# Computing the modulation in quarters beside the first two projection groups, with GpSimd taking two of sixteen row sums

## The chip, the cores and the metric

One core of a Trainium2 chip. The metric is the device time of one launch in microseconds (us), the median of several executions. The engines are named as the profile names them: PE (TensorE), DVE (VectorE), ACT (ScalarE), POOL (GpSimd), SP (the queue that issues most transfers).

## What is computed

Two transformer blocks over 256 tokens of width 2048. The change touches the start of the first and two details later. All weights are float32 in HBM, and every matrix product is to have float32 precision.

```python
mod = silu(c) @ ada_w + ada_b                  # c: 2048 values, ada_w: 2048 x 6144
shift, scale, gate = split(mod, 3)
h = rms_norm(x, norm_g) * (1.0 + scale) + shift
proj = h @ w_in                                # 2048 x 9296, in groups of 512 columns
```

Then follow rotations, a recurrence (forget gates from the first 1024 columns computed), an index score (16 heads of 64), a top-64 selection, attention, an output projection, and a second block with a long convolution, attention and a feed-forward layer.

## The kernel before

**Products.** `Gemm` cuts each product in groups of 512 columns, each group in chunks of 512 rows (1 MB, one transfer from SP into one of the four places of `raw`), each chunk in two parts. A part is numbered through the whole kernel. For each part ACT rounds the weights (`high`, L399), DVE takes the remainder (`low`, L408), and PE makes 12 matmuls of 512 columns (`multiply_group`, L430): three products of halves for two row tiles and two token tiles. `w_hi` holds four parts, so ACT and DVE are at most four parts ahead of PE. Two pairs of PSUM banks (`ps`) are used in turns by even and odd groups; a group starts when the group two before it has been read out. Work beside the products is written as generators that yield the number of the part at which they may go on (`GATE_AT`, `INDEX_AT`, `TAPS_AT` and others), and `Spare` hands it out after each part.

**Modulation (the start).** Shift and scale are 4096 columns, so `n_ada` = 8 steps g of 512 columns, in order of columns. Each step streams 2048 rows of `ada_w` as four 1 MB chunks c = 0..3 through the same four places of `raw` (SP, L2199 and L2203; `ada_free` says when a place is free). A chunk holds four row sums: a weight row tile times four columns of `c_sig`. PE makes nine of the sixteen itself (c = 0, c = 2 and the first of c = 3, stationary operand one column wide, L511), DVE makes the other seven into `mod_part` (L1149, L1151), and PE adds that up over the partitions with a column of ones. ACT copies the row out (`mod_row`, L1857) and PE turns it into columns with four tiny matmuls (128 columns of a row each). DVE has `before_products` beside it: the rotation angles and their sine, the normalised rows (`normalise`, L1023), the lower bounds of the forget gate (`lb`, L1113 to L1133). PE turns three units of normalised rows (L523) between steps.

After the last step DVE adds the bias (L1163), ACT makes the input tiles `h_hi` from PSUM with scale and shift (`tile_of_first`, L1793), DVE their lower halves (`low_of_first`, L967), and PE starts with part 0; parts 0 to 7 are group 0, 8 to 15 group 1. Only when the last `ada_w` chunks are used does SP load `w_in`.

**Later.** `gate_row` streams the gate's third of `ada_w` in 16 chunks from ACT's queue, beside the products, 64 operations on DVE (L1182). The index scores are 16 steps of two matmuls over 64 partitions (`kiT`, `qiT`); even steps use partitions 0 to 63, odd ones 64 to 127. The filter taps are eight matmuls over 64 partitions, four on the lower half, then four on the upper one, two at each part. The recurrence's `inside` makes three such matmuls per head, two on the lower and then one on the upper 64 partitions. GpSimd makes only the filter's first layer (L2265), which starts when the recurrence is over.

## Time and profile before

| what | value |
|---|---|
| median of 3 runs (lowest, highest) | 2101.46 us (2100.26, 2109.39) |
| the profiled execution itself | 2106.29 us |
| its span in the trace | 2104.5 us |
| mean granted clock of PE | 0.986 |
| busy: PE, DVE, ACT, POOL | 2058.0, 1302.7, 927.1, 383.0 us |
| moved by DMA | 408.47 MB, mean 194 GB/s |

Times inside the trace are counted from the start of the span. The busy time of an engine is no limit by itself: the stage in which it waits has to be looked up.

### The profile page before, as it was taken

What the parts mean: (1) busy time and instruction counts of PE and PEld (TensorE: products, weight loads), DVE (VectorE), ACT (ScalarE), POOL (GpSimd) and SP (SyncE); (2) the same over time, 40 slices, a digit from 0 to 9 for tenths busy, and PEclk for the clock granted to TensorE, in tenths of its full rate; (3) what the DMA queues carried; (4) which work ended last, traced back from release to release, by engine and by line L of the source; (5) the groups of instructions that cost most, each with busy time, mean ns of one, the idle gap of its engine ahead of it and who ended that gap; (6) DMA issues with size and microseconds to landing.
All of it is one profiled execution on the core that took longest, in us unless ns stands there. A gap on an engine that the chain in (4) does not pass through costs nothing.

```text
span 2104.5 us, 23568 instructions
## 1 busy us (share of the span) xinstructions
PE 2058.0 (98%) x9245; PEld 1623.4 (77%) x9245; DVE 1302.7 (62%) x1651; ACT 927.1 (44%) x1224; POOL 383.0 (18%) x588
## 2 busy tenths in 40 slices
PE   6989999999999999999999999999999999999999
PEld 1268787777887888786788888888888888878887
DVE  4857667798666678865765666554544544444443
ACT  1165523455654544354454434554444444433332
POOL 0000002999999950000000000000000000000000
PEclk9999989999999999999999999999999999999999
DMA  9967557555565675554435555555555555546554
GB/s 353 344 236 249 199 185 220 180 171 164 171 213 196 200 231 180 160 163 130 138 129 186 187 198 180 180 194 187 191 188 186 194 186 194 194 166 199 186 195 160
DMA packets 205683, 408.47 MB, mean 194 GB/s; under 512 B 10826, under 2 KB 12163, under 8 KB 204931
## 3 DMA queue, kind: packets, MB, share of 16 engines
q1 hardware_dynamic: 190480, 376.07, 54.1%
q10 hardware_dynamic: 13332, 24.40, 3.4%
q0 software_dynamic: 1760, 6.49, 1.5%
q8 instruction: 73, 1.20, 0.2%
q14 instruction: 38, 0.31, 0.0%
HBM read 404.83 MB, written 2.10 MB: 193 GB/s over the span
## 4 chain that ended last, share of the span: by engine, by line
PE 91%; DVE 6%; DMA 2%; issue 1%; ACT 0%; ACTq 0%; SPq 0%; DVEq 0%
PE ps L430 81%; PE pm L511 6%; DMA raw<-in_ada_w 2%; DVE raw_lo L408 1%; PE ps L511 1%; PE pm L523 1%; DVE mod_part L1151 1%; PE pm L575 1%; PE pm L888 0%; DVE gate L1182 0%; DVE xtmp L1351 0%; DVE sc_i L1268 0%; DMA rows_b<-in_hgrn_norm_g 0%; DVE proj L1328 0%; PE pm L710 0%
## 5 line engine op out<-in xcount | busy, mean ns | idle before, releaser
L408 DVE TENSOR_TENSOR raw_lo<-raw,w_hi 128x1024 fp32r<-128x1024 f32 (+1 forms) x648 | 799.9, 1238 | 597.6 <-ACT w_hi L399 589.0
L399 ACT ACTIVATE w_hi<-raw 128x1024 fp32r<-128x1024 f32 (+1 forms) x648 | 680.1, 1050 | 821.0 <-PE ps L430 796.3
L430 PE MATMUL ps<-w_hi,h_hi 128*128 128x512 f32 (+1 forms) x2336 | 941.3, 403 | 12.5 <-DVE raw_lo L408 6.4
L430 PE MATMUL ps<-w_hi,h_lo 128*128 128x512 f32 (+1 forms) x2336 | 912.5, 391 | 0.0
L430 PE MATMUL ps<-raw_lo,h_hi 128*128 128x512 f32 (+1 forms) x2336 | 911.2, 390 | 0.0
L430 PEld LDWEIGHTS ps<-w_hi,h_hi 128*128 128x128 f32 x2336 | 442.8, 190 | 117.3 <-issue 13.0
L430 PEld LDWEIGHTS ps<-raw_lo,h_hi 128*128 128x128 f32 x2336 | 443.3, 190 | 93.3 <-issue 7.7
L430 PEld LDWEIGHTS ps<-w_hi,h_lo 128*128 128x128 f32 x2336 | 442.2, 189 | 93.4
L2265 POOL TENSOR_TENSOR proj<-proj 128x128 f32<-128x128 f32 x264 | 177.8, 679 | 12.9
L2265 POOL TENSOR_TENSOR proj<-proj,w1T 128x128 f32<-128x128 f32 x165 | 102.8, 631 | 11.4 <-DMA proj<-in_z 4.2
L430 PE MATMUL ps<-w_hi,hid_hi 128*128 128x512 f32 x256 | 100.6, 393 | 2.0 <-DVE raw_lo L408 2.0
L430 PE MATMUL ps<-raw_lo,hid_hi 128*128 128x512 f32 x256 | 100.3, 392 | 0.0
L430 PE MATMUL ps<-w_hi,hid_lo 128*128 128x512 f32 x256 | 100.2, 391 | 0.0
L2244 POOL DMA_DIRECT2D proj<-in_z x22 | 14.1, 645 | 344.4 <-DVEq L1246 338.7
L511 PE MATMUL ps<-raw,c_sig 128*1 128x512 f32 x144 | 70.2, 638 | 6.7 <-DMA raw<-in_ada_w 6.5
L430 PEld LDWEIGHTS ps<-w_hi,hid_hi 128*128 128x128 f32 x256 | 48.3, 189 | 12.3 <-DVE raw_lo L408 2.2
L511 PEld LDWEIGHTS ps<-raw,c_sig 128*1 128x1 f32 x144 | 11.5, 87 | 59.5 <-issue 47.0
L430 PEld LDWEIGHTS ps<-w_hi,hid_lo 128*128 128x128 f32 x256 | 48.5, 189 | 10.1
L430 PEld LDWEIGHTS ps<-raw_lo,hid_hi 128*128 128x128 f32 x256 | 48.4, 189 | 10.0
L1182 DVE SCALAR_TENSOR_TENSOR gate<-proj,c_sig,gate 128x512 f32<-128x512 f32 x64 | 49.1, 767 | 1.9
L2265 POOL TENSOR_TENSOR proj<-h3T,proj 128x128 f32<-128x128 f32 x66 | 48.9, 742 | 0.0
L1151 DVE SCALAR_TENSOR_TENSOR mod_part<-raw,c_sig,mod_part 128x512 f32<-128x512 f32 x48 | 36.0, 750 | 10.2 <-DMA raw<-in_ada_w 8.6
(308 smaller groups left out, 1183.5 us busy)
## 6 DMA issues: line engine op xcount, KB each, us to landing
raw<-in_w_in SPq DMA_DIRECT2D x140, 1024.0 KB, 5.2
raw<-in_w_ffn_gate SPq DMA_DIRECT2D x44, 1024.0 KB, 5.2
raw<-in_w_ffn_up SPq DMA_DIRECT2D x44, 1024.0 KB, 5.2
raw<-in_w_ffn_down SPq DMA_DIRECT2D x44, 1024.0 KB, 5.2
raw<-in_ada_w SPq DMA_DIRECT2D x32, 1024.0 KB, 7.7
raw<-in_w_out SPq DMA_DIRECT2D x32, 1024.0 KB, 5.2
proj<-in_ada_w ACTq DMA_DIRECT2D x16, 1024.0 KB, 5.3
raw<-in_w_br_hyena SPq DMA_DIRECT2D x8, 1024.0 KB, 5.2
```

Source lines behind the costliest of these rows:

```text
L399: nc.scalar.activation(w_hi[:, p % HRING, :, 0:gm.width(j)], raw[:, k % RING, e:e + HT, 0:gm.width(j)], ACT.Copy).then_inc(hi_done, 1)
L408: nc.vector.tensor_tensor(raw_lo[:, k % RING, e:e + HT, 0:gm.width(j)], raw[:, k % RING, e:e + HT, 0:gm.width(j)], w_hi[:, p % HRING, :, 0 ...
L430: mm = nc.tensor.matmul(ps[pair][:, t, 0:gm.width(j)], l[:, tok], r[:, i, 0:gm.width(j)], start=(k == 0 and q == 0), stop=(k == kt - 1 and ...
L511: return nc.tensor.matmul(o, l, r, start=start, stop=stop, **kw)
L523: i = nc.tensor.transpose(b[:, ((k % 2) * TT + t) * P:((k % 2) * TT + t + 1) * P], src[:, t, k * P:k * P + P], ident[:])
L575: i = nc.tensor.transpose(b[:, o:o + P], src[:, t, h * HD:h * HD + HD], ident[:])
L1151: i = v.scalar_tensor_tensor(mod_part[:, g % 2], raw[:, c, k], w_, mod_part[:, g % 2], ALU.mult, ALU.add)
L1182: x = v.scalar_tensor_tensor(acc, gate_raw[i % 2][:, k], c_sig[:, CK * c + k:CK * c + k + 1], acc, ALU.mult, ALU.add)
L2244: pool.dma_start(z_k[e % 2][half * HID:half * HID + HID], z.partition_broadcast(HID)).then_inc(sig(f"z_in{e % 2}"), 16)
L2265: g.tensor_tensor(o, x, y, op).then_inc(sig("sum_step"), 1)
```

## The change

The `w_in` groups 0 and 1 advance together: for each quarter q of the 2048 inputs, the steps g = 2q (shift) and g = 2q + 1 (scale) of the modulation are computed, and then the four parts of quarter q of both groups. The parts are renumbered (`part` with `together`: 0, 1 of group 0, 2, 3 of group 1, and so on).

- `ada_w` chunks go to four places of their own in `proj` (`ada_raw`); SP issues the `w_in` chunk of group 0 behind c = 0 and that of group 1 behind c = 1 of each odd g.
- Row sums of a step: PE five of sixteen (c = 0 and the first of c = 2), POOL two (the first two of c = 1: two multiplications and an addition of 128x512), DVE nine and one addition of POOL's sum.
- PE's queue, for g even: sums of c = 0, turn the previous quarter's two rows (eight tiny matmuls), sum of c = 2, the ones matmul behind `mod_parts`, two parts of that quarter. For g odd: c = 0, a part, c = 2, a part, the ones matmul; in the last step both parts come after it. The whole normalised input is turned at g = 2 and copied by ACT into `h1_raw`.
- DVE's queue: for g even, the columns of the quarter (`columns_of`) behind c = 1, a `low_of_first` behind c = 2 and c = 3; for g odd, the `low` of four parts behind c = 3. `before_products` has lost the angles; they go as `rotation_angles` beside groups 2 and 3. The gate's chunks start at part 22 instead of 12 and end at 78 as before.
- The index matmuls of two steps are issued together, alternating between the lower and the upper 64 partitions; the taps alternate too.

```diff
-ADA_PE = 1
+PE_C2 = 1
+POOL_C1 = 2
-GATE_AT = [12 + 22 * i // 5 for i in range(4 * ADA_GATE)]
+GATE_AT = [22 + 56 * i // 15 for i in range(4 * ADA_GATE)]
...
+        if self.together and j < 2 and n < self.parts:
+            return self.n0 + 2 * PARTS * (n // PARTS) + PARTS * j + n % PARTS
...
+        ada_raw = [proj[:, 1, o:o + CK * GW].rearrange("p (k n) -> p k n", k=CK) for o in (A_Q, A_V, R_Q, R_I)]
...
+            if c % 2 == 0:
+                sp.wait_ge(ada_used, 2 * (g - 1) + 1 + c // 2)
+            if c:
+                sp.wait_ge(mod_parts, 3 * (g - 1) + c)
+            if c == 1:
+                sp.wait_ge(sig("pool_sums"), g)
...
             for g in range(n_ada):
+                q = g // 2 - 1
+                if g == 2:
+                    pe.wait_ge(sig("h1_rows"), 1)
+                    for u in range(KT // 2):
+                        b = bank(pe, ("h1", u), "a")
...
+                row_sums(g, 0, CK, sums)
+                if q >= 0:
+                    if g % 2 == 0:
+                        turn_modulation(q, mods)
+                    elif g < n_ada - 1:
+                        early_part(4 * q + 2)
+                row_sums(g, 2, PE_C2, sums)
+                if q >= 0 and g % 2 and g < n_ada - 1:
+                    early_part(4 * q + 3)
+                pe.wait_ge(mod_parts, 3 * g + 3)
+                mm(sums[0:1, :], ones[:, 0:1], mod_part[:, g % 2], start=False, stop=True).then_inc(filled, 1)
+                if q >= 0:
+                    if g % 2 == 0:
+                        early_part(4 * q)
+                        early_part(4 * q + 1)
+                    elif g == n_ada - 1:
+                        early_part(4 * q + 2)
+                        early_part(4 * q + 3)
+            q = n_ada // 2 - 1
+            turn_modulation(q, bank(pe, ("mods", q), "v"))
+            for p in range(2 * g_in.parts - 4, 2 * g_in.parts):
+                early_part(p)
...
-                    for j in range(IDX_H // 2):
-                        yield INDEX_AT[1 + t] + j
+                    for j in range(0, IDX_H // 2, 2):
+                        yield INDEX_AT[1 + t] + j + 1
...
+                        for q in range(2):
+                            for r in range(2):
+                                part = slice(IDX_D * r, IDX_D * r + IDX_D)
+                                m = mm(b[r][:, q * SEQ:q * SEQ + nk], qiT[part, j + q, t * P:t * P + P], kiT[part, 0:nk])
...
-                    t, n = i // 4, i % 4
+                    t, n = i % TT, i // TT
...
+                for c, k0 in ((1, POOL_C1), (2, PE_C2), (3, 0)):
+                    dve.wait_ge(ada_landed[c], 16 * (g + 1))
...
+                            if last:
+                                dve.wait_ge(sig("pool_sums"), g + 1)
+                                v.tensor_tensor(mod_part[:, g % 2], mod_part[:, g % 2], pool_part[g % 2], ALU.add).then_inc(sig("pool_added"), 1)
...
+                    if q >= 0 and g % 2 == 0:
+                        if c == 1:
+                            columns_of(q)
+                        else:
+                            low_of_first(2 * q + c - 2)
+                    if g % 2 and c == 3:
+                        for p in range(4 * (g // 2), 4 * (g // 2) + (2 if g == n_ada - 1 else 4)):
+                            low_of(p)
+                    early.step(g, 3.0 if g < 2 else 1.2)
+            for p in range(2 * g_in.parts - 2, 2 * g_in.parts):
+                low_of(p)
+            columns_of(n_ada // 2 - 1)
+            for u in (KT // 2 - 2, KT // 2 - 1):
+                low_of_first(u)
...
+            groups(g_in, (2, 3), None, ((chain, 1e9), (angles, 1.6), (gate_work, 1.0)))
...
-            for c in range(RING):
-                sp.dma_start(raw[:, c], ada_v[:, CK * c:CK * c + CK, 0:GW]).then_inc(landed[c], 16)
-            for g in range(1, n_ada):
+            for g in range(n_ada):
+                o = D * (g % 2) + GW * (g // 2)
                 for c in range(RING):
-                    ada_free(sp, g, c)
-                    sp.dma_start(raw[:, c], ada_v[:, CK * c:CK * c + CK, GW * g:GW * g + GW]).then_inc(landed[c], 16)
+                    if g:
+                        ada_free(sp, g, c)
+                    sp.dma_start(ada_raw[c], ada_v[:, CK * c:CK * c + CK, o:o + GW]).then_inc(ada_landed[c], 16)
+                    if g % 2 and c < 2:
+                        load(sp, g_in, c, g // 2)
...
+            def row_part(g_):
+
+                pool.wait_ge(ada_landed[1], 16 * (g_ + 1))
...
+                for k, o in ((0, pool_part[g_ % 2]), (1, pool_part[2])):
+                    g.tensor_tensor(o, ada_raw[1][:, k], c_sig[:, CK + k:CK + k + 1].to_broadcast([P, GW]), ALU.mult).then_inc(sig("pool_step"), 1)
+                pool.wait_ge(sig("pool_step"), 2 * (g_ + 1))
+                g.tensor_tensor(pool_part[g_ % 2], pool_part[g_ % 2], pool_part[2], ALU.add).then_inc(sig("pool_sums"), 1)
```

## Rows read from the trace of the kernel before

**Rows 1.** The page: busy time of the engines over the span.
```profile
PE 2058.0 (98%) x9245; PEld 1623.4 (77%) x9245; DVE 1302.7 (62%) x1651; ACT 927.1 (44%) x1224; POOL 383.0 (18%) x588
```

**Rows 2.** Windows: length; PE, PEld, DVE, ACT, POOL busy; PE clock, DMA share, GB/s.
```profile
40.00:80.00 40.00, 36.18 (x108) 9.56 (x108) 34.33 (x56) 7.02 (x8) 0.00 (x0) 1.00 1.03 372
...
90.00:100.00 10.00, 10.00 (x23) 2.06 (x22) 6.48 (x6) 0.35 (x1) 0.00 (x0) 0.85 0.58 203
...
160.00:210.00 50.00, 50.00 (x226) 40.80 (x225) 35.94 (x38) 26.42 (x28) 0.00 (x0) 0.97 0.72 248
...
290.00:300.00 10.00, 10.00 (x60) 8.26 (x60) 7.38 (x12) 2.30 (x3) 0.00 (x0) 0.50 0.37 127
...
360.00:410.00 50.00, 46.32 (x193) 35.56 (x192) 45.08 (x51) 20.88 (x35) 46.85 (x60) 1.00 0.65 209
```

**Rows 3.** Timeline of PE at the start: start, us, instruction, idle before it.
```profile
63.69 3.59 PE L511 MATMUL ps<-raw,c_sig 128*1 128x512 f32 x8
...
99.54 1.05 PE L511 MATMUL ps<-ones,mod_row 1*128 1x1 f32 x8
...
100.52 0.66 PE L523 MATMUL pm<-ident,hbuf 128*128 128x128 f32 x4
...
111.70 1.02 PE L511 MATMUL ps<-mod_part,ones 128*1 128x512 f32 x2 [0.69 <-DVE mod_part L1151]
...
120.61 0.79 PE L430 MATMUL ps<-w_hi,h_hi 128*128 128x512 f32 x1 [5.43 <-DVE h_lo L967]
...
123.33 0.60 PE L430 MATMUL ps<-w_hi,h_hi 128*128 128x512 f32 x1
```

**Rows 4.** The chain that ended last: one part of a group.
```profile
125.53 2.76 PE ps L430 x12
```

**Rows 5.** Timeline of DVE at the start.
```profile
36.90 2.33 DVE L1151 SCALAR_TENSOR_TENSOR mod_part<-raw,c_sig,mod_part 128x512 f32<-128x512 f32 x3 [1.10 <-DMA raw<-in_ada_w]
...
45.98 2.61 DVE L1023 TENSOR_SCALAR hbuf<-x_res,hs 128x2048 f32<-128x2048 f32 x2
...
91.12 3.35 DVE L1126 RECIPROCAL xtmp<-xtmp 128x512 f32<-128x512 f32 x1
...
109.32 2.33 DVE L1151 SCALAR_TENSOR_TENSOR mod_part<-raw,c_sig,mod_part 128x512 f32<-128x512 f32 x3 [2.10 <-DMA raw<-in_ada_w]
...
114.70 0.19 DVE L1163 TENSOR_TENSOR mod_cols<-ps,cols 128x32 f32<-128x32 f32 x1 [3.05 <-PE ps L511]
...
115.25 4.63 DVE L408 TENSOR_TENSOR raw_lo<-raw,w_hi 128x1024 fp32r<-128x1024 f32 x4
...
119.80 0.76 DVE L967 TENSOR_TENSOR h_lo<-xtmp,h_hi 128x256 fp32r<-128x256 f32 x2
```

**Rows 6.** Timeline of ACT: an input tile, and the read-out of group 1.
```profile
117.04 0.54 ACT L1793 ACTIVATE xtmp<-pm,mod_cols,g_col 128x256 f32<-128x256 f32 x1
...
167.85 1.03 ACT L1888 ACTIVATE proj<-ps 128x1024 f32<-128x1024 f32 x1 [1.60 <-PE ps L430]
```

**Rows 7.** The page: transfers of w_in, KB each, median us from issue to landing.
```profile
raw<-in_w_in SPq DMA_DIRECT2D x140, 1024.0 KB, 5.2
```

**Rows 8.** Timeline of PE: matmuls over 64 partitions; each matmul is two instructions.
```profile
321.74 0.71 PE L511 MATMUL pm<-proj 64*128 64x128 f32 x6
...
423.99 0.71 PE L511 MATMUL pm<-kiT,qiT 64*128 64x128 f32 x4
...
481.26 1.13 PE L511 MATMUL pm<-kiT,qiT 64*128 64x256 f32 x4
...
875.52 1.98 PE L511 MATMUL pm<-gate,h3T 64*128 64x512 f32 x4
```

**Rows 9.** Groups by line: POOL; then DVE within 200 to 340 us.
```profile
L2265 POOL TENSOR_TENSOR proj<-proj,w1T 128x128 f32<-128x128 f32 x165 | 102.8, 631 | 11.4 <-DMA proj<-in_z 4.2
...
L1182 DVE SCALAR_TENSOR_TENSOR gate<-proj,c_sig,gate 128x512 f32<-128x512 f32 x36 | 27.0, 749 | 1.1
```

**Rows 10.** Groups by line: the same DVE line within 360 to 400 us.
```profile
L1182 DVE SCALAR_TENSOR_TENSOR gate<-proj,c_sig,gate 128x512 f32<-128x512 f32 x8 | 7.1, 890 | 0.2
```

More of the change, by code:

```diff
@@ L128, in part, with done @@
     def part(self, j, n=0):
+        if self.together and j < 2 and n < self.parts:
+            return self.n0 + 2 * PARTS * (n // PARTS) + PARTS * j + n % PARTS
         return self.n0 + self.parts * j + n
+    def done(self, j):
+        return self.part(j, self.parts - 1) + 1
     def end(self):
@@ L205, in build @@
         sn_rope = sb("sn_rope", [P, 5, 2 * TT * 96], F32, st)
+        mod_row = sb("mod_row", [P, 2, GW], F32, st)
+        mod_part = sb("mod_part", [P, 2, GW], F32, st)
         st.close()
@@ L334, in build @@
         landed = [sem(f"landed{i}") for i in range(RING)]
+        ada_landed = [sem(f"ada_landed{i}") for i in range(RING)]
         ada_used = sem("ada_used")
@@ L555, in _, with row_sums @@
-            pe.wait_ge(sig("mod_read"), n_ada + 2)
-            for j in range(4 * (n_ada - 1), 4 * n_ada):
-                m = mm(mod_bank[:, j:j + 1], mod_row[0:1, j * P:j * P + P], ones[0:1, 0:1])
-            m.then_inc(sig("mod_turned"), 1)
+            def row_sums(g, c, n, b):
+                pe.wait_ge(ada_landed[c], 16 * (g + 1))
+                for k in range(n):
+                    m = mm(b[0:1, :], c_sig[:, CK * c + k:CK * c + k + 1], ada_raw[c][:, k], start=(c == 0 and k == 0), stop=False)
+                m.then_inc(ada_used, 1)
@@ new lines, in turn_modulation, with early_part @@
+            def turn_modulation(q, b):
+                for r in range(2):
+                    drained(("mod", 2 * q + r))
+                    for i in range(CK):
+                        m = mm(b[:, CK * r + i:CK * r + i + 1], mod_row[0:1, r, i * P:i * P + P], ones[0:1, 0:1])
+                m.then_inc(filled, 1)
+            def early_part(p):
+                n = 2 * (p // 4) + p % 2
+                pe.wait_ge(sig("first_lo"), n + 1)
+                multiply_part(pe, g_in, p % 4 // 2, n, halves)
@@ L735, in _ @@
             beside = Chains(mixer, gate_sum)
-            def turn_h1(n):
-                if n + 3 < KT // 2:
-                    turn_unit("h1", hbuf, n + 3)
-                drained(("h1", n))
-            for j in range(g_in.groups):
-                multiply_group(pe, g_in, j, halves, turn_h1 if j == 0 else None, beside if j else None)
+            for j in range(2, g_in.groups):
+                multiply_group(pe, g_in, j, halves, None, beside)
             multiply(pe, g_o, halves, made("mix"), beside)
@@ L1162, in _ @@
[L1162 to L1171 removed]
+                            dve.wait_ge(mod_parts, 3 * g + c)
@@ L1418, in _ @@
             gate_sum = Spare(gate_sums())
+            groups(g_in, (2, 3), None, ((chain, 1e9), (angles, 1.6), (gate_work, 1.0)))
+            assert angles.over
             beside = ((chain, 1e9), (gate_sum, 1e9), (gate_work, 1.0), (head_work, 1.2))
-            groups(g_in, range(1, g_in.groups), None, beside)
+            groups(g_in, range(4, g_in.groups), None, beside)
             assert gate_work.over and head_work.over and gate_sum.over
@@ L2035, in _ @@
             beside = ((chain, 1e9), (norm_work, 1.2), (gate_work, 1e9))
-            groups(g_in, range(1, g_in.groups), read_in, None, beside)
+            groups(g_in, range(2, g_in.groups), read_in, None, beside)
             assert norm_work.over and gate_work.over
```

279 lines of the change are left out of this document (145 added, 134 removed).

## The prediction, made before the changed kernel was run

> **What bounds the kernel now.** The page comes first: PE is busy for 2058.0 of 2104.5 us [rows 1], so outside the places where PE waits only fewer or shorter matmuls can save anything. The windows say where it waits. From 40 to 80 us the DMA share is 1.03 at 372 GB/s, with PE busy for 36.2 and DVE for 34.3 of 40 us: the modulation runs at the rate of the transfers, and both engines are nearly full beside it [rows 2]. Between 90 and 100 us the share falls to 0.58 while PE is busy throughout at a clock of 0.85: there PE's sums hold the places of the ring. The timeline gives the end of the stage: DVE gets the last chunk at 109.3 us [rows 5], PE's first product starts at 120.6 after 5.43 us of idleness, and it runs at the lower clock until 123.3 [rows 3]; ACT reads group 1 out at 167.85 [rows 6]. So the start costs 120 us ahead of the products, and groups 0 and 1 end at 167.7. Everything behind that is PE's, but for a stretch like 360 to 410 us, where PE is busy for 46.3 and DVE for 45.1 of 50 us: DVE is late there [rows 2].
>
> **Prices.** One 1 MB chunk at 372 GB/s takes 2.8 us [rows 2]; alone, it lands 5.2 us after its issue [rows 7]. Four row sums on PE take 3.6 us, one 0.9, the ones matmul 1.0, the four tiny turning matmuls 1.0, a transposed unit 0.66 [rows 3]; a part is 2.76 us [rows 4]. On DVE three sums are 2.33 us, a `low` 1.16, a `low_of_first` 0.76, the columns with their gaps some 0.5 (from 114.70 to 115.25), the rows' normalisation 2.61, half a reciprocal 1.65 [rows 5]. An ACT tile operation lasts 0.54 us, and four make a unit, 1.85 us as they overlap a little [rows 6]. The addition of POOL's sum is not in the trace: I take 0.7 us, between nothing and the 0.75 of a three-operand one [rows 9], so that DVE's four sums and the addition are 3.8 us, and 4.1 with POOL beside them.
>
> **DMA.** In place of 4 chunks a step there are 10 a pair of steps (8 of `ada_w`, 2 of `w_in`): 28.2 us a pair. Nothing is removed, 8 MB are moved ahead of the last `ada_w` chunk: 8 x 2.8 = 22.5 us more of transfers. In return up to ten of the sixteen parts, 27.6 us, lie beside them. The floor of the exchange is therefore a gain of a few us and not of 27.
>
> **The first pair.** DVE's last sums of step 1 start at 36.9 now [rows 5]; two `w_in` chunks ahead put that at 42.5. The early work behind c = 2 (normalisation, reciprocal and a 1.16 us maximum, 4 us) holds DVE from 42.3 to 46.3, so the sums end at 50.4 and the ones matmul at 51.4. Then PE turns all eight units at once (6 us, paced by ACT's copies) and does c = 0 of step 2: S = 61.
>
> **A pair in steady state.** I follow PE from the end of the c = 0 sums of an even step (S) to the same point one pair on. PE turns eight tiny matmuls (2.0), DVE makes the columns (0.5), the three sums of c = 2 (2.33), a `low_of_first` (0.8) and the sums of c = 3 (4.1); PE makes the ones matmul (1.0), two parts (5.5), c = 0 of the odd step (3.6), a part (2.76), a sum (0.9), a part (2.76), the ones matmul (1.0) and c = 0 again (3.6): 30.8 us. Ahead of the even ones matmul PE has been idle for some 7 us. After 5.43 us of idleness it needed 2.7 us for what takes half of that [rows 3], so 1.3 us come on top: 32.1 us. This is longer than the 28.2 us of the transfers, so **the chain PE, DVE, PE sets the pair and no longer the DMA**; `columns_of` stands ahead of the c = 2 sums on DVE, and c = 0 of the odd step, which SP waits for to reload, stands behind two parts on PE. S for step 6 is 61 + 64.2 = 125.2.
>
> **The end of the stage.** Steps 5 to 7 also carry the lower bounds' reciprocals, two of 1.65 us in this chain: mod_parts of step 6 at 138.2, ones and two parts with the clock 146.1, c = 0 and c = 2 of step 7 at 150.5 (the last chunk, issued at 138.2, lands at 143.4 and is summed by 147.5, so it does not decide). Then ones (151.5), parts 10 and 11 (157.0), `high` and `low` of part 15 which stand ahead of the columns (159.2), columns, an input tile, its lower half (162.3), and the four parts of the last quarter: groups 0 and 1 end at 173.3, **5.6 us later than now**. SP's reload of `raw` behind them waits for parts 10 to 15 in turn and lands ahead of its use.
>
> **POOL.** Its 128x128 operation takes 0.63 us [rows 9]; for 512 columns that bounds it by 0.63 and 2.5 us. I take 1.4, by the ratio of DVE's 512 and 128 columns in the same class of work being about two: 4.2 us for three, 7.6 at the upper end. Either lies inside a step of 16 us and delays no reload. What it costs is DVE's speed: the same DVE sum took 749 ns with POOL idle and 890 ns with POOL at work [rows 9, 10], 19% more. POOL works for a quarter of a step, early in it, hence my 0.3 us a step. The Trainium skill's GPSIMD Engine Reference, Key points, says that POOL shares its SBUF interfaces with VectorE and contends with instructions that have two SBUF inputs, which is nearly everything DVE does here; the trace agrees. If all sums of the chain paid 19%, it would be 1.2 us a pair and 3.6 us in all, so 9 and not 5.6 us.
>
> **Beside groups 2 and 3.** The angles come to DVE here, 10.9 us by the shares in their generator. DVE is busy for 35.9 of 50 us between 160 and 210 [rows 2], so 14 us are free, and the first gate chunks (operations of 0.75 us) leave it. It fits, barely: 1 us, bounds 0 and 3. The gate's sixty-four operations then stand closer together (16 chunks in 56 parts, not 66); where DVE already is late, 360 to 410 us, that is one or two operations of 0.89 us: 1 us, bounds 0 and 2.
>
> **The 64-partition matmuls.** Two matmuls of 128 columns (four instructions) last 0.71 us and two of 256 columns 1.13, so 0.42 is for columns and 0.29 fixed. Three matmuls of the recurrence, of which the last uses the other 64 partitions, are six instructions and also last 0.71 us, where 0.92 would be due one after the other [rows 8]: the third was hidden. By that, joined steps cost what one costs: the index saves 4 x 0.71 + 4 x 1.13 less tails, some 6.6 us, the taps 4 x (1.98 - 1.13), 3.4 us: 10 us. The lower bound is the fixed part alone, eight times 0.29, 2.3 us. PE is the bound at both places, so it counts.
>
> **Sum.** +5.6 + 1 + 1 - 10 = -2.4 us against the profiled execution (span 2104.5, time 2106.29, itself 4.8 above the median). Taken off the median of 2101.46: **2099 us**. A change under 0.5%, 10.5 us, is about what a measurement of this kernel can't tell from none.
>
> **Rivals.**
> - *The transfers keep the pace* (0.20). The engines' chain slips beside them, each pair takes 28.2 us: last chunk at 42.5 + 84.6 = 127.1, then 4.1 + 1.0 + 5.5 + 2.2 + 0.5 + 1.85 + 0.8 + 11.0 = 26.9 us, end at 154, 13.7 us earlier; in all -22 us: 2080. For it: the share of 1.03 now. Against: DVE's columns wait for PE in each pair, and nothing in the order written out lets either pass.
> - *Matmuls over alternate halves don't overlap* (0.13): 2.3 us saved in place of 10, 2107. For it: only one pair of three shows it.
> - *The clock stays down in the stage* (0.12), slower. PE now waits in short stretches every pair; granted half speed lasted beyond them (0.85 at 90 to 100 us with PE busy throughout, 0.50 for all of 290 to 300 [rows 2]). A pair holds some 24 us of PE's work. My sum has 2.7 us of it at the lower clock. Each further 2 us cost 1; if half of the work is at the lower clock, 5 us a pair beyond mine come on, 15 in all, 2114. It turns slower by 0.5% from some 11 us a pair at half speed.
> - *The overlap fails* (0.05): a part's `high` waits for a part that PE issues behind the sums, so that the parts run as a block. Up to ten parts come back, and 22.5 us of transfers stay: 2120 to 2125.
> - *My forecast* (0.50), its own range 2092 to 2107.
>
> **Numbers.** Faster by over 0.5%: the first rival, and the lower edge of my forecast, 0.27. Slower: the clock and the failed overlap in most of their cases, 0.12. Within: 0.61. The range reaches from the first rival to the middle of the third, 2080 to 2113.
>
> **What would show it.** Right: S near 61 and 93, groups 0 and 1 read out at 172 to 175 us, DMA share about 0.9 from 60 to 140 us, PE idle ahead of the ones matmul of even steps for 5 to 8 us and DVE idle ahead of `columns_of`; index rows of eight instructions at about 0.71 and 1.13 us; DVE sums at 0.75 to 0.89. Wrong: a read-out ahead of 160 us, a share of 1.0 throughout, joined rows at 1.1 and 2.0 us, or a waits view in which POOL's sum holds DVE.

## The result and the profile after

The changed kernel takes 2120.9 us (median of nine runs, 2114.67 to 2124.03), the kernel before 2104.34 on the same chips (nine runs, 2098.67 to 2109.39). The ratio is 1.0075, 95% interval 1.006 to 1.0089: **slower by three quarters of a per cent**, where 2099 us and no measurable change were forecast, and outside the range of 2080 to 2113. The profiled execution took 2117.41 us with a span of 2115.6, so the two traces differ by 11.1 us and the medians by 16.5. The profile of before is 2 us above its median, that of after 3.5 below; the account below is of the 11.1.

The page of the changed kernel: busy times, and the group of PE's products that waits.
```profile
PE 2028.8 (96%) x9181; PEld 1615.9 (76%) x9181; DVE 1334.2 (63%) x1683; ACT 932.5 (44%) x1232; POOL 415.0 (20%) x612
...
L440 PE MATMUL ps<-w_hi,h_hi 128*128 128x512 f32 (+1 forms) x2336 | 945.1, 405 | 20.4 <-DVE raw_lo L423 15.8
```
PE is busy for 29 us less than in [rows 1]: 64 instructions fewer are 32 row sums at 0.9 us. Yet the span is longer, so PE is idle for 86.8 us in place of 46.5. DVE is busy for 31.5 us more. By design it has two sums and an addition more in each step than before, which are 18 us (16 sums of 0.75 us, and 6.2 us of additions); where the rest comes from is the subject of the second experiment.

The timeline of PE from 50 to 170 us, only the rows of the modulation and of the waits:
```profile
52.04 1.87 PE L529 MATMUL pm<-mod_part,ones 128*1 128x512 f32 x2 [10.84 <-DVE mod_part L1218]
...
62.15 1.94 PE L529 MATMUL pm<-ones,mod_row 1*128 1x1 f32 x16
...
71.41 1.87 PE L529 MATMUL pm<-mod_part,ones 128*1 128x512 f32 x2 [6.37 <-DVE mod_part L1218]
...
95.19 1.94 PE L529 MATMUL pm<-ones,mod_row 1*128 1x1 f32 x16
...
104.44 1.87 PE L529 MATMUL pm<-mod_part,ones 128*1 128x512 f32 x2 [6.36 <-DVE mod_part L1218]
...
128.69 1.94 PE L529 MATMUL pm<-ones,mod_row 1*128 1x1 f32 x16
...
139.60 1.86 PE L529 MATMUL pm<-mod_part,ones 128*1 128x512 f32 x2 [8.02 <-DVE mod_part L1218]
...
153.77 1.02 PE L529 MATMUL pm<-mod_part,ones 128*1 128x512 f32 x2 [0.68 <-DVE mod_part L1218]
...
166.03 0.80 PE L440 MATMUL ps<-w_hi,h_hi 128*128 128x512 f32 x1 [3.71 <-DVE h_lo L1016]
```
The starts of the `ones,mod_row` rows are the prediction's S: 62.15, 95.19 and 128.69, forecast 61, 93.1 and 125.2. The pairs last 33.0 and 33.5 us, not 32.1, and PE waits 6.4 to 8.0 us ahead of each even ones matmul, which takes 1.87 us after that idleness and 1.02 in the odd steps, after a wait of 0.68 us or none.

ACT's timeline has the read-out of group 1, which answers to 167.85 in [rows 6]:
```profile
180.07 1.03 ACT L1980 ACTIVATE proj<-ps 128x1024 f32<-128x1024 f32 x1 [1.09 <-PE ps L440]
```
So groups 0 and 1 end 12.2 us later than before; 5.6 was forecast. Windows of the same kernel, with columns as in [rows 2]:
```profile
60.00:140.00 80.00, 59.25 (x201) 29.36 (x199) 62.62 (x79) 25.91 (x38) 16.30 (x12) 0.84 0.85 306
...
202.00:210.00 8.00, 7.93 (x32) 6.53 (x32) 7.83 (x10) 3.25 (x3) 0.00 (x0) 0.79 0.27 80
```
The columns are the length, the busy times of PE, its weight loads, DVE, ACT and POOL, then the clock, the DMA share and GB/s. The DMA share of 0.85 shows that the transfers no longer pace the stage; the engine that is fullest is DVE. The granted clock of 0.84 was 0.91 in the same window before.

**Where the time came from.** I subtracted the start of the same part's first product in the timelines of PE (part 16: 167.7 before, 179.9 after). Worked out from the traces, us later than before:
```
part                       0     8    16    24    84   120   236   252   end
the changed kernel     -47.4  -4.5 +12.2 +17.1 +15.7 +16.4 +15.4 +11.2 +11.1
without POOL's sums    -48.9  -7.8  +6.3  +9.9 +10.3 +11.6  +9.0  +6.4  +6.4
```
The second row is that of an experiment below. The early start is real (part 0 is 47.4 us ahead), and by part 16 all of it is gone. 4.9 us more go in group 2. Over the index steps (parts 84 to 120) the offset first falls, to +11.0 at part 112, and is back at +16.4 by part 120, so nothing net is gained. 4.2 come back in the stretch with the taps (236 to 252). How these stand to the terms forecast comes after the experiments.

### The profile page after: what moved, and what is told of

Its sections match the earlier page's. It is cut to its first block, busy times and chain, and to the rows that moved or that the text cites. A ratio compares the mean times of both kernels' runs of the same rounds, so it can differ in the third digit from the quotient of the medians.

```text
span 2115.6 us, 23544 instructions
## 1 busy us (share of the span) xinstructions
PE 2028.8 (96%) x9181; PEld 1615.9 (76%) x9181; DVE 1334.2 (63%) x1683; ACT 932.5 (44%) x1232; POOL 415.0 (20%) x612
## 4 chain that ended last, share of the span: by engine, by line
PE 89%; DVE 8%; DMA 1%; issue 1%; ACT 1%; ACTq 0%; SPq 0%; DVEq 0%
PE ps L440 79%; PE pm L529 7%; DVE raw_lo L423 2%; DVE mod_part L1218 1%; DMA proj<-in_ada_w 1%; PE pm L541 1%; PE pm L628 1%; DVE sc_i L1338 0%; PE pm L938 0%; DVE xtmp L1421 0%; DVE gate L1252 0%; ACT w_hi L414 0%; DMA rows_b<-in_hgrn_norm_g 0%; DVE proj L1163 0%; PE pm L585 0%
## 5 line engine op out<-in xcount | busy, mean ns | idle before, releaser
L1218 DVE SCALAR_TENSOR_TENSOR mod_part<-proj,c_sig,mod_part 128x512 f32<-128x512 f32 x64 | 52.9, 827 | 9.6 <-DMA proj<-in_ada_w 7.6
L529 PE MATMUL pm<-mod_part,ones 128*1 128x512 f32 x16 | 12.4, 869 | 38.5 <-DVE mod_part L1218 38.5
L529 PE MATMUL pm<-proj,c_sig 128*1 128x512 f32 x80 | 40.5, 642 | 8.6 <-DMA proj<-in_ada_w 8.6
```

The source lines that it names most:

```text
L529: return nc.tensor.matmul(o, l, r, start=start, stop=stop, **kw)
L1218: i = v.scalar_tensor_tensor(mod_part[:, g % 2], ada_raw[c][:, k], w_, mod_part[:, g % 2], ALU.mult, ALU.add)
```

## The experiments

Each ratio below is against the kernel before on the same chip. Single ratios carry some 0.0015 either way, so the traces decide on terms of a few us, and where the two disagree it is said.

### Alternate taps alone

```diff
-                    t, n = i // 4, i % 4
+                    t, n = i % TT, i // TT
```
This is the kernel before with that one edit, on PE and on DVE.

> The kernel before with one edit: the eight filter-tap matmuls alternate between the lower and the upper 64 partitions. If alternate halves overlap, the stretch with the taps is 3.4 to 4 us shorter in the trace (part 236 to 252) and four instructions that lasted 1.98 us last about 1.1; total 2100. Rival, that the 4.1 us that the changed kernel won in that stretch come from somewhere else (other buffers, the clock): no difference, 2104.

Measured: 2103.42 us (ten runs), ratio 1.0001 (0.9986 to 1.0017). The timeline of PE in it:
```profile
873.17 1.13 PE L511 MATMUL pm<-gate,h3T 64*128 64x512 f32 x4
```
1.13 us in place of 1.98 [rows 8]: the halves overlap. Four such groups are 3.4 us, which this ratio does not show. So it was run again:

> The kernel of before_taps once more, with more rounds, since its trace was 5.7 us shorter in the stretch with the taps and its median was not. If the 3.4 us of four steps (1.98 to 1.13 us) stay, the ratio is 0.998 to 0.9985. If something later takes them back in unprofiled executions, it is 1.000 again.

Measured: 2101.32 us, ratio 0.9983 (0.9966 to 1.0), which is the 3.4 us forecast, at the edge of what twelve runs can tell. The traces are clearer. From the first of the four groups to the transposes behind the last it is 22.45 us in the kernel before and 19.1 in every kernel with alternate taps: 3.4 us each time. The stretch from part 236 to 252 is longer and differs less evenly, by 5.7 us in the first run and 2.5 in the second, because behind the taps the clock was low for a while before (0.86 from 925 to 950 us), not at all in the first run (1.00) and again in the second (0.86). Two kernels below differ by the taps as well.

### POOL's row sums

```diff
-POOL_C1 = 2
+POOL_C1 = 0
-                                dve.wait_ge(sig("pool_sums"), g + 1)
-                                v.tensor_tensor(mod_part[:, g % 2], mod_part[:, g % 2], pool_part[g % 2], ALU.add).then_inc(sig("pool_added"), 1)
```
SP's wait for POOL and the calls of POOL's `row_part` are gone too; DVE makes eleven of the sixteen sums.

> The changed kernel with POOL's two row sums of each step back on DVE, its addition gone. Theory 1 (the chain through PE, DVE and the low clock sets the stage): DVE has two sums more and one addition less, 0.8 us a step, but its c = 1 sums, 2.8 to 3.0 us for two beside POOL, go at 0.75 each again, so four take as long as two; groups 0 and 1 end within 1.5 us of 179.9, total 2119 to 2122. Theory 2 (POOL's slowing of DVE is what the stage lost against the forecast): the sums behind it also get faster, groups 0 and 1 end at 174 to 176, total 2116 or less. Theory 3 (POOL does help): the stage is 4 us or more longer.

Measured: 2112.21 us (four runs), ratio 1.0053 (1.0038 to 1.0068). Its row in the table above stands 5.9 us below the changed kernel's at part 16. **With more sums on DVE, the stage is shorter.** Its S are 61.40, 94.10 and 125.83, near the forecast's 61, 93.1 and 125.2.

The groups of DVE by line within 20 to 165 us, first of the changed kernel:
```profile
L1218 DVE SCALAR_TENSOR_TENSOR mod_part<-proj,c_sig,mod_part 128x512 f32<-128x512 f32 x60 | 49.9, 832 | 7.5 <-DMA proj<-in_ada_w 5.6
...
L423 DVE TENSOR_TENSOR raw_lo<-raw,w_hi 128x1024 fp32r<-128x1024 f32 x16 | 20.6, 1320 | 7.8 <-ACT w_hi L414 7.7
...
L1211 DVE TENSOR_SCALAR mod_part<-proj,c_sig 128x512 f32<-128x512 f32 x7 | 7.9, 1126 | 13.9 <-DMA proj<-in_ada_w 13.9
...
L1216 DVE TENSOR_TENSOR mod_part<-mod_part,proj 128x512 f32<-128x512 f32 x8 | 6.2, 781 | 0.3
```
The same groups without POOL's sums:
```profile
L1214 DVE SCALAR_TENSOR_TENSOR mod_part<-proj,c_sig,mod_part 128x512 f32<-128x512 f32 x74 | 55.4, 749 | 9.1 <-DMA proj<-in_ada_w 6.9
...
L421 DVE TENSOR_TENSOR raw_lo<-raw,w_hi 128x1024 fp32r<-128x1024 f32 x16 | 19.0, 1222 | 9.8 <-ACT w_hi L412 9.7
...
L1209 DVE TENSOR_SCALAR mod_part<-proj,c_sig 128x512 f32<-128x512 f32 x7 | 3.2, 456 | 15.8 <-DMA proj<-in_ada_w 15.8
```
Add them: 84.6 us of DVE with POOL's help, 77.6 without. POOL takes 14 sums, 10.5 us; the addition gives 6.2 back; the rest, 84.6 - (77.6 - 10.5 + 6.2) = 11.3 us, is what DVE loses while POOL works beside it. The mean of 832 ns hides where. The timelines of both engines of the changed kernel, in step 4, DVE first:
```profile
92.00 2.04 DVE L423 TENSOR_TENSOR raw_lo<-raw,w_hi 128x1024 fp32r<-128x1024 f32 x1 [2.61 <-ACT w_hi L414]
93.97 1.26 DVE L1211 TENSOR_SCALAR mod_part<-proj,c_sig 128x512 f32<-128x512 f32 x1
95.26 1.64 DVE L1218 SCALAR_TENSOR_TENSOR mod_part<-proj,c_sig,mod_part 128x512 f32<-128x512 f32 x1
...
91.92 1.04 POOL L2370 TENSOR_TENSOR proj<-proj,c_sig 128x512 f32<-128x512 f32 x1 [15.10 <-issue]
...
92.92 2.02 POOL L2370 TENSOR_TENSOR proj<-proj,c_sig 128x512 f32<-128x512 f32 x1
...
95.02 1.32 POOL L2372 TENSOR_TENSOR proj<-proj 128x512 f32<-128x512 f32 x1
```
and the same DVE work without POOL:
```profile
90.91 1.22 DVE L421 TENSOR_TENSOR raw_lo<-raw,w_hi 128x1024 fp32r<-128x1024 f32 x1 [2.61 <-ACT w_hi L412]
92.05 0.48 DVE L1209 TENSOR_SCALAR mod_part<-proj,c_sig 128x512 f32<-128x512 f32 x1
92.57 2.33 DVE L1214 SCALAR_TENSOR_TENSOR mod_part<-proj,c_sig,mod_part 128x512 f32<-128x512 f32 x3
```
Beside POOL the `low` takes 2.04 in place of 1.22 us, the first sum 1.26 in place of 0.48, the next 1.64 in place of some 0.77: 1.7 to 2.6 times as long, for as long as POOL's three operations of 512 columns last. The rows read as if the two engines took turns: the `low` ends at 94.04, 1.08 us after POOL's first product (92.96), POOL's second product then ends 0.90 later (94.94) and has taken 2.02 us where the first took 1.04, and each DVE operation ends a fraction of its own time after POOL's. That they take turns is my reading of the times; no run tests it. Not every DVE operation is slowed. The first reciprocal of step 6 lies beside POOL's operations, which last from 125.36 to 129.72, and takes as long as the next one with POOL idle, 1.75:
```profile
127.41 1.74 DVE L1163 RECIPROCAL proj<-proj 128x256 f32<-128x256 f32 x1
```

Is it contention, or the waits and the addition? The next kernel keeps POOL's products, its sum (in steps 0 to 6) and SP's wait (which costs SP 0.3 us in all), but DVE makes all eleven sums and uses none of it. POOL's part of the edit, against the changed kernel:
```diff
-            for g_ in range(n_ada):
+            for g_ in range(n_ada - 1):
                 row_part(g_)
```

> The kernel after_nopool (DVE makes all eleven sums), but in steps 0 to 6 POOL makes its two products and their sum all the same, into memory that nobody reads; SP's reload of c = 1 waits for them as in the changed kernel. If POOL's work slows DVE's, groups 0 and 1 end 5 to 8 us later than the 173.9 of after_nopool, and the c = 1 sums beside POOL's work take 1.3 to 1.4 us in place of 0.49 and 0.75; total 2118 to 2121. If the changed kernel lost the time by its addition and the wait for POOL's sum, it ends at 173 to 175, total 2112.

Measured: groups 0 and 1 end 11.6 us later than before, not 6.3, and DVE's rows within 20 to 165 us are:
```profile
L1216 DVE SCALAR_TENSOR_TENSOR mod_part<-proj,c_sig,mod_part 128x512 f32<-128x512 f32 x74 | 63.3, 856 | 4.4 <-DMA proj<-in_ada_w 2.2
...
L423 DVE TENSOR_TENSOR raw_lo<-raw,w_hi 128x1024 fp32r<-128x1024 f32 x16 | 20.4, 1321 | 6.3 <-ACT w_hi L414 6.1
...
L1211 DVE TENSOR_SCALAR mod_part<-proj,c_sig 128x512 f32<-128x512 f32 x7 | 7.1, 1019 | 16.4 <-DMA proj<-in_ada_w 16.4
```
The same instructions as without POOL now take 90.8 us, 13.2 more. So in the traces **POOL's mere presence costs the stage 5.3 us**, near all of the 5.9. The medians don't confirm it: 2115.47 us is again a ratio of 1.0053 (1.0037 to 1.0068), because the kernel before was slower there (2105.5, against 2100.96 beside the kernel without POOL's sums). By ratio, POOL's sums cost 0.0022 in all, with overlapping intervals. I take the traces, where both the durations and the end of the stage agree. They don't stand alone either. Of the kernels in this document that keep the changed kernel's order of parts, the five with POOL at work (this one, the changed one, and those with the angles, the index and the fill edited) start part 16 10.7 to 13.4 us behind before's, and the three without it 5.5 to 6.4. And one pair of whole times is clear of its intervals: with the angles spread in both, 1.0053 (1.0033 to 1.0074) with POOL's sums and 1.0011 (0.9998 to 1.0024) without, the second also with the index as before, which by itself gained nothing.

### The angles over three groups

```diff
-            groups(g_in, (2, 3), None, ((chain, 1e9), (angles, 1.6), (gate_work, 1.0)))
+            groups(g_in, (2, 3, 4), None, ((chain, 1e9), (angles, 0.8), (gate_work, 1.0)))
```


> The changed kernel with the rotation angles spread over groups 2 to 4 at half the share a part (0.8 in place of 1.6). If DVE's load by the angles makes the 5 us that the changed kernel loses between parts 16 and 24, the wait of 3.0 us at 202 us goes and part 24 starts 3 to 5 us earlier; total 2117. Rival, that those 5 us are the low clock carried over from the start and the read-out of both groups at once: 0 to 1 us, total 2121.

Measured: 2112.74 us (four runs), ratio 1.0053 (1.0033 to 1.0074). Its parts 16 and 24 both stand 10.7 us behind before's; the changed kernel's stand 12.2 and 17.1 behind. The 4.9 us of group 2 are gone, the other 1.5 differ ahead of any edit and are spread between executions. The traces of the other kernels agree: with the angles crowded into groups 2 and 3 the six that were taken lose 3.6 to 6.0 us between parts 16 and 24, and the five with the angles spread lose 0.0. The 3.6 is that of the kernel without POOL's sums, so POOL isn't needed for this loss. (The profile of this run is another 6 us shorter where a low clock between parts 52 and 56 came out shorter; that isn't the edit's.)

What the angles do there, in the timeline of PE and the chain of waits of the changed kernel:
```profile
202.07 0.50 PE L440 MATMUL ps<-w_hi,h_hi 128*128 128x512 f32 x1 [2.97 <-DVE raw_lo L423]
```
```profile
182.38 1.22 DVE raw_lo L423
183.60 1.15 DVE proj L1267
...
184.78 0.57 DVE sn_rope L996
...
199.22 0.76 DVE gate L1252
...
200.79 1.24 DVE raw_lo L423
...
202.07 2.33 PE ps L440 x6
```
From 182.38 to 202.03 us the chain is DVE without a break: remainders, `proj` work of the forget gate, angles, gate. DVE falls behind, PE waits 2.97 us and then runs at a clock of 0.79 over 8 us (the window above), which is 1.7 us more: together 4.7 of the 4.9 us. The 0 to 3 us forecast counted the wait and not what the wait does to the clock.

### The index matmuls as before

PE's order (one step after the other) and the yields of ACT and DVE go back to those of the kernel before:
```diff
-                    for j in range(0, IDX_H // 2, 2):
-                        yield INDEX_AT[1 + t] + j + 1
+                    for j in range(IDX_H // 2):
+                        yield INDEX_AT[1 + t] + j
```


> The changed kernel with the index matmuls, and the part numbers of ACT and DVE for them, as before. Theory 1 (DVE is the bound from part 92 to 120, so what PE saves there comes back as a wait, and the shift by one part makes a new one of 4.7 us): without the edit the offset to the kernel before stays within 1 us from part 84 to part 128, where the changed kernel goes from +15.7 down to +11.0 and up to +16.4; total 2120, no difference. Theory 2 (the edit saves the 6.6 us forecast, and the wait at part 116 has another cause): the offset rises by 4 to 6 us to +20, total 2126.

Measured: 2121.96 us (four runs), ratio 1.009 (1.0073 to 1.0107), beside the changed kernel's 1.0075. Its parts stand 21.1 us behind before's at 84 and 21.0 at 120, and never more than 0.3 from that between them. The changed kernel's 15.7 and 16.4 are nearly the same at both ends, with the dip to 11.0 between. So the saving is made and then lost. The joined steps themselves last just what was forecast:
```profile
442.42 0.71 PE L529 MATMUL pm<-kiT,qiT 64*128 64x128 f32 x8
...
494.75 1.13 PE L529 MATMUL pm<-kiT,qiT 64*128 64x256 f32 x8
```
Eight instructions in the time of four [rows 8]. Its waits within 425 to 545 us (us in total, times, longest) and the chain ahead of the longest:
```profile
PE ps L440 <- DVE raw_lo L423: 8.3, 4, 4.7
```
```profile
518.07 0.61 DVE sc_i L1338
...
521.70 1.71 DVE xtmp L1421 x2
...
524.57 1.37 DVE raw_lo L423
```
With the index as before the same wait is 1.7 us, once. Ahead of the longest wait the chain is DVE's, from 513.45 to 525.94 us, busy for 12.6 of 13 us from 513 to 526: the scores, the search for the top 64 and the rotations stand ahead of the remainder that PE waits for. So 6.6 us less on PE came back as 6.6 us more of waits, 8.3 less 1.7. DVE's share over the whole stretch, 101.6 of 120 us busy, would not have told this by itself (see the taps below). The two kernels' whole times don't differ beyond their intervals.

### The parts moved into the waits

PE waits 6 to 8 us ahead of the even ones matmul, and makes two parts in a row behind it. Here the last two parts of the quarter before go ahead of that matmul, and the first two stand around the sums of the odd step:
```diff
                 row_sums(g, 2, PE_C2, sums)
-                if q >= 0 and g % 2 and g < n_ada - 1:
-                    early_part(4 * q + 3)
+                if q >= 0 and g % 2:
+                    early_part(4 * q + 1)
+                if q >= 1 and g % 2 == 0:
+                    early_part(4 * q - 2)
+                    early_part(4 * q - 1)
```
The rounding and the remainders of these parts move with them.

> The changed kernel with the parts in other places of PE's queue: the first two parts of a quarter around the sums of the following odd step, the last two in the wait ahead of the ones matmul of the next even step. Nothing is added or removed. Theory 1 (the chain sets the pair, 33 us, with 6 to 8 us of PE idle in it and the clock falling): PE's idle time is filled, the clock stays up, a pair takes 28 to 30 us, groups 0 and 1 end at 167 to 171, total 2109 to 2113. Rival (the transfers or DVE set the pair): the pair stays at 33 us, total 2120.

Measured: 2119.51 us (four runs), ratio 1.0084 (1.0058 to 1.0109), no gain in the whole time. Its timeline of PE:
```profile
62.83 1.94 PE L529 MATMUL pm<-ones,mod_row 1*128 1x1 f32 x16
...
89.48 1.94 PE L529 MATMUL pm<-ones,mod_row 1*128 1x1 f32 x16
...
114.47 1.87 PE L529 MATMUL pm<-mod_part,ones 128*1 128x512 f32 x2 [4.44 <-DVE mod_part L1217]
...
121.27 1.94 PE L529 MATMUL pm<-ones,mod_row 1*128 1x1 f32 x16
```
The first pair is 26.7 us, shorter than the 28.2 that the transfers were priced at; the next is 31.8 again, with PE waiting for DVE, which from step 5 on has the reciprocals of the lower bounds. So the order fills PE's gap once, and then DVE is late. Even so the stage is shorter: part 16 stands 8.2 us behind before's, 4.0 less than in the changed kernel. Behind it this profile has more low clock: the granted clock is 0.83 from 195 to 225 us and 0.76 from 280 to 330, where the changed kernel's is 0.89 and 0.83. That is some 5 us, and the end is 1.3 us later than the changed kernel's. The second of these clocks differs between profiles whatever the order of the parts (0.76 to 0.93), so the whole time of four runs says little about the order itself.

### Matmuls that keep the clock up

Matmuls with a column of zeros as weights fill PE's waits, `FILL = (0, 6, 5, 0, 5, 0, 5, 3)` of them in the eight steps; they add nothing to the sums:
```diff
                 row_sums(g, 2, PE_C2, sums)
+                for _ in range(FILL[g]):
+                    mm(sums[0:1, :], zcol[:, 0:1], x_res[:, 0, 0:GW], start=False, stop=False)
```


> The changed kernel with extra matmuls behind PE's c = 2 sum (stationary operand zero, so they add nothing): six in step 1, five in steps 2, 4 and 6, three in step 7. They fill the waits ahead of the ones matmul. Theory 1 (the low clock costs the stage some 2 us a pair): the clock stays at 1.00 through the stage, the first matmuls of parts 0, 4 and 8 start every 0.23 us, groups 0 and 1 end 5 to 8 us ahead of 179.9, total 2114. Rival (the clock falls in the stage, but DVE sets the chain, so that the lost time is waited for anyway): end within 2 us of 179.9, total 2120.

Measured: 2120.01 us (four runs), ratio 1.0085 (1.0069 to 1.0101). A window of it:
```profile
100.00:110.00 10.00, 7.93 (x28) 4.14 (x27) 7.36 (x11) 6.15 (x8) 2.22 (x2) 1.00 1.05 389
```
The granted clock holds at 1.00 (2.4 GHz) from 60 to 140 us but for a hundredth, where it was 0.84, and both pairs shrink to 30.6 us. But the stage ends 13.4 us late, not earlier. Where the gain goes can be seen in step 6. PE comes to it 2.7 us earlier than in the changed kernel (S of 125.94 and 128.69), but DVE does not: its reciprocal, 127.41 in the changed kernel above, starts here at
```profile
127.43 1.74 DVE L1170 RECIPROCAL proj<-proj 128x256 f32<-128x256 f32 x1
...
137.54 1.54 DVE L1223 TENSOR_TENSOR mod_part<-mod_part,proj 128x512 f32<-128x512 f32 x1
...
139.11 1.41 DVE L1225 SCALAR_TENSOR_TENSOR mod_part<-proj,c_sig,mod_part 128x512 f32<-128x512 f32 x1
```
and then POOL's products of step 7, which start at 137.49, fall on the last two operations of step 6 (1.54 and 1.41 us; 0.69 and 0.75 in the changed kernel). So the ones matmul of step 6 starts 1.0 us later than there, after 7.46 us of waiting. The low clock in this stage is a cost that lies beside DVE's.

### Without POOL, the angles and the index together

> The changed kernel without POOL's sums, with the angles spread over groups 2 to 4 and the index matmuls as before; the quarters, the two groups together and the alternating taps stay. If the gains of the single edits add up (8.7 and 8.2 us by the medians), this is 2121 - 17 = 2104, the same as the kernel before: the quarters then bring nothing of themselves. If POOL and the angles cost the same time (DVE's), it is 2110.

Measured: 2104.99 us (twelve runs), ratio 1.0011 (0.9998 to 1.0024). Parts 16, 24 and the end stand 6.4, 6.4 and -0.1 us to before. POOL's sums and the crowded angles account for the measurable part of the slowing; what is left is the stage's own 6.4, against the taps and stretches of low clock that differ between the profiles.

With the taps as before as well:

> Only the quarters and the two groups together, in the order of the changed kernel: POOL's sums on DVE, the angles over groups 2 to 4, index and taps as before. By the traces the start costs 6 us (part 16 at +6.4 in the kernel that also had the taps) and nothing comes back later: 2107 to 2110 against 2103. Rival (the quarters gain of themselves, and the taps of the kernel before this one gave nothing, as in before_taps): 2103 to 2105.

Measured: 2108.17 us (twelve runs), ratio 1.0018 (1.0005 to 1.0031). Part 16 stands 5.5 us behind before's, part 120 4.2 and the end 2.3: before's profile has more low clock behind this stage. This is the exchange by itself (modulation in quarters, ten of sixteen parts early, four more sums a step on DVE): a small loss, as expected for this run. Against the kernel above the alternate taps are worth 3.2 us in medians, 1.5 by the ratios, whose intervals overlap, and 3.4 in the traces (22.45 and 19.1 us for the groups above).

### The same with the parts in the waits, and the lower bounds earlier

With the reordering of the experiment on waits:

> The same with the parts in PE's waits (the order of after_gap). Theory 1 (with POOL gone DVE keeps up, and PE's queue sets the pair): pairs of 28 to 29 us in place of 32, groups 0 and 1 end at 164 to 168, total 2096 to 2100, below both kernels. Rival (DVE sets the pair, as it did in the second half of after_gap): the same as without that order, 2104 to 2108.

Measured: 2100.64 us (twelve runs), ratio 0.9985 (0.9971 to 0.9998). Part 16 stands 1.4 us behind before's, not 6.4. So the order pays 5.0 us here, where it paid 4.0 with POOL at work. What holds it still is DVE from step 5 on; the ones matmuls of steps 4 and 5:
```profile
94.16 1.02 PE L527 MATMUL pm<-mod_part,ones 128*1 128x512 f32 x2
...
110.00 1.86 PE L527 MATMUL pm<-mod_part,ones 128*1 128x512 f32 x2 [3.18 <-DVE mod_part L1211]
```
so the lower bounds' exponential and reciprocals start two steps earlier, where DVE still has gaps:
```diff
-                yield 5
+                yield 3
                 dve.wait_ge(sig("lb_exp"), 1)
...
-                    if g == 4:
+                    if g == 2:
                         act.wait_ge(sig("lb_less"), 2)
```


> The fastest kernel so far (parts in PE's waits, no POOL, angles spread, index as before, taps alternating) with the exponential of the lower bounds at step 2 and their reciprocals on DVE from step 3 on, where DVE waits for chunks, in place of step 5 on. Theory (after the first pair DVE's queue sets the pace, and PE waits 3 to 4 us for its sums in steps 5 to 7): these waits shrink, groups 0 and 1 end 2 to 5 us ahead of 169.1, total 2097. Rival (the transfers of steps 3 and 4 are then late instead): no difference, 2101.

Measured: 2098.27 us (twelve runs), ratio **0.9973 (0.9961 to 0.9985)**, the fastest of all and faster than both kernels, by a quarter of a per cent against the kernel before. Part 16 starts 0.6 us ahead of before's, and the trace ends 6.8 ahead, of which 3.4 are the taps. The waits did not simply shrink: ahead of the ones matmuls of steps 6 and 7 they go from 1.54 and 3.60 us to none and 1.78, but in steps 3 and 4, where there were none, they are now 1.66 and 1.79. Its window, beside the changed kernel's above:
```profile
60.00:140.00 80.00, 67.20 (x234) 32.15 (x232) 67.38 (x94) 27.50 (x40) 0.00 (x0) 0.94 0.93 341
```
PE is busy for 67.2 and not 59.3 of 80 us, and the DMA share is 0.93: the transfers have come near again. The 2.4 us between the last two kernels are within their intervals.

## Why the prediction was wrong

The sum was -2.4 us; the traces give +11.1. Forecast and measured, term by term, in us (measured from the table of parts):
```
term                                      forecast   measured
start, groups 0 and 1 end                   +5.6       +12.2   (part 16)
angles beside groups 2 and 3                +1.0        +4.9   (16 to 24)
gate's operations closer together           +1.0        -1.4   (24 to 84)
index steps joined                          -6.6        +0.7   (84 to 120)
taps alternate                              -3.4        -4.2   (236 to 252; 3.4 of it the taps)
all else                                     0          -1.1   (120 to 236, 252 to the end)
sum                                         -2.4       +11.1
```

- **What held.** The chain from PE to DVE to PE, not the transfers, sets the pair. Without POOL's sums the S measured are within 1.0 us of those forecast, and the quarters by themselves lose 5.5 us by part 16 where 5.6 were forecast. That this fits so well is partly luck: the forecast was for the kernel with POOL's sums and holds 1.0 us a pair for the addition and POOL's slowing, which these kernels don't have, and it allowed too little for the clock (below). PE waits 6.4 to 8.0 us ahead of the even ones matmul, where 5 to 8 were forecast; the last chunk does not decide (DVE makes its sums of step 7 without a wait); joined rows last 0.71 and 1.13 us and the taps 1.13. The rival of unoverlapped halves (0.13) is out, and so are that of the transfers keeping pace (share 0.85, not 1.0) and that of the failed overlap (part 0 starts 47.4 us early and parts stand singly between the sums).
- **POOL's contention: the term mis-sized.** "19% more... for a quarter of a step, early in it, hence my 0.3 us a step." The 19% is what POOL's 128-column operations cost a DVE sum [rows 9, 10]. Beside its 512-column operations DVE took 1.7 to 2.6 times as long, and POOL is at work for 3.3 to 4.3 us in each step (in step 4 two products in 3.02 us, the sum in 1.32). Over the stage that is 11.3 us of DVE's time, 1.6 for each of the seven steps in the window, not 0.3. Even the bound of 3.6 us, "if all sums of the chain paid 19%", was below the 5.3 that the unused sums cost the stage. The size of POOL's own operations was right: 1.0 to 1.6 us each, but for two of 2.02, where 1.4 was taken. The direction stood in the Trainium skill's GPSIMD Engine Reference, Key points (POOL contends with DVE instructions that have two SBUF inputs or run in a two-port mode); the trace agrees in that; the page gives no size, and in this trace the instruction hit hardest is the first sum, 0.48 to 1.26 us, which has one 512-column input. It takes 0.48 us alone for the columns that cost a multiply-and-add 0.75, so it may be in that two-port mode; no run here shows it. The reciprocal, also with one input, is not slowed.
- **The angles: mis-sized.** 14 us free on DVE against 10.9 us of angles was right as a total over 50 us. But the 19.7 us from 182.38 to 202.03 have no gap, since the angles stood there with the forget gate's rows and the gate's sums. A total over a window says nothing of the order within it. And the wait it made cost low clock behind it, which "bounds 0 and 3" had left out. The upper bound was passed.
- **The index: the wrong engine.** "PE is the bound at both places, so it counts" fails for the index. The prediction named the stretch where DVE is late (45.1 of 50 us busy from 360 to 410) for the gate, but never asked the same of the index's own stretch. There DVE is busy for 101 of 120 us in both kernels (415 to 535 us before, 425 to 545 after), PE came up against it as soon as it had 6.6 us less to do, and the waits took them. At the taps the same kind of saving stayed whole. DVE's share is no lower there (38.5 of 45 us from 860 to 905 us, 85% as at the index), but PE is busy for all of the 45 us: it never waits. So it is the waits, not the share, that tell the two places apart.
- **The clock: right as a cost, wrong as a rival.** 0.84 of full speed from 60 to 140 us is lower than the 1.3 us a pair allowed. Yet the rival "the clock stays down" is not what made the kernel slower: holding the clock at 1.00 took 2.4 and 2.9 us off the pairs and nothing off the whole. The Trainium skill's page TensorE: Matmul & The Clock Gate, HAM oscillation, tells of kernels in which repeated waits bring the clock down each time; this trace agrees, with 1.87 us for the ones matmul after each wait of 6 us or more and 1.02 without one, and a granted clock of 0.84. What the low clock takes from PE here, PE would otherwise spend waiting for DVE.
- **The gate's density** was no cost that the traces show; the -1.4 holds a stretch of low clock near 300 us that both kernels have, and that is shorter in the changed one (0.80 before and 0.83 after from 280 to 330 us, 1.5 us), so it isn't a price.

The slow side had been given 0.12, all of it to the clock and the overlap. The two mechanisms that made the kernel slower were both in the sum, with bounds from the nearest rows. Those rows were of another size (128 columns) and of another kind (a total). The prediction also took 0.5% for about what can't be told from none; nine runs of each kernel gave an interval of 0.15% either way.

**Still open:** whether DVE and POOL really take turns, and which mode of DVE's is slowed. The whole times show less than the traces: the kernel with POOL's unused sums has the same ratio as the one without them. The medians differ by 5 us more than the profiles, because each profile lies off its median (before's above, after's below); the times of single executions go with their granted clock (for the kernel before in one session 2099.05 us at 0.989 and 2111.46 at 0.984), and why the clock differs between executions is not known. That the cost of the angles is wait plus clock is read from one trace, and not from a run that held the clock there.

## What to carry to other kernels

Before handing a share of DVE's work to POOL, add up DVE's time with POOL at work on operations of that very size: the help was 10.5 us, the addition 6.2, and the contention 11.3. A saving on one engine counts only where that engine has no one to wait for, and this is to be looked up for each place: in the waits and the chain of that place, since a busy share of 85% on the other engine took a saving back at one place and not at the other. And an exchange that opens waits on PE should fill them with parts already due; by the end of the stage that was worth 4.0 us with POOL at work and 5.0 without.

## What the runs showed of the hardware

- Three POOL operations of 128x512 float32 stretch most DVE operations beside them: 1.22 to 2.04 us for a subtraction of 128x1024, 0.48 to 1.26 for a scaled copy of 128x512, 0.77 to 1.64 for a multiply-and-add. A reciprocal of 128x256 beside them is not stretched (1.74 us). POOL's product is stretched in turn, 1.04 to 2.02 us beside the subtraction. With 128 columns POOL's operations stretch the multiply-and-add from 749 to 890 ns only.
- Four matmuls over 64 partitions, two on each half and in alternate order, take what two take: 0.71 us at 128 columns, 1.13 at 256; and two of the taps' 512-column matmuls over alternate halves take 1.13 us where two over the same half took 1.98. This is as the Trainium skill's TensorEngine Tiling (Array Packing), Key Properties, has it, that tiles run independently; only the size is from here.
- With PE's waits filled by matmuls of zero weight, the granted clock was 0.99 from 60 to 140 us, and 0.84 without them; the kernel was no faster for it.
